# Scan with its bands two rounds ahead, and projections that begin with the receptance, in a hybrid RWKV-7 / attention step

## What is computed

```python
dx = centred_shift(h) - h                      # 0.5 * (left + right neighbour) - h
xr, xw, xk, xv, xa, xg = [h + dx * mu[n] for n in range(6)]
r = heads(xr @ w_r); k_raw = xk @ w_k; v = heads(xv @ w_v); g = sigmoid(xg @ g1) @ g2
for d in range(2):                             # both directions, 16 heads of 64
    decay, a, k_d = ...                        # from xw, xa and k
    def step(S, inp):
        sa = einsum('bhij,bhj->bhi', S, a_t)
        S = S * w_t[..., None, :] + v_t[..., :, None] * k_t[..., None, :] + sa[..., :, None] * b_t[..., None, :]
        return S, einsum('bhij,bhj->bhi', S, r_t)
```

## Time and profile before

| | us |
|---|---|
| median of 3 timed runs | 1508.85 |
| lowest and highest of them | 1502.84, 1514.56 |
| the profiled execution, its own time | 1497.86 |
| span of the profiled execution, first to last instruction | 1496.1 |
| PE busy | 1276.4 (85%) |
| DVE, POOL, ACT busy | 527.0, 387.4, 325.4 |
| mean granted PE clock | 0.92 of 2.4 GHz |

### The profile page before, as it was taken

How to read it: one execution, slowest core, us unless ns; L and a number is a source line. 1 busy time by engine, 2 the same in 40 slices (tenths; PEclk the granted TensorE clock), 3 DMA queues, 4 the chain that set the end, 5 groups by cost and what they waited for, 6 DMA issues and landing times. The chain is left out here.

```text
span 1496.1 us, 21672 instructions
## 1 busy us (share of the span) xinstructions
PE 1276.4 (85%) x8627; PEld 894.2 (60%) x8627; DVE 527.0 (35%) x1159; ACT 325.4 (22%) x801; POOL 387.4 (26%) x708
## 2 busy tenths in 40 slices
PE   4699979999999888799577798979997794888897
PEld 2355845877888777535344455655685452555656
DVE  2800066556655654363510011320025525011115
ACT  2100153332222220031311111111116403111111
POOL 0100065554455432100024223000006601233310
PEclk9899988999999988589789999979997996999997
DMA  9922034766566224206369977847220073877752
GB/s 327 305 94 103 1 122 152 218 212 193 161 212 210 55 62 138 102 1 232 124 256 401 366 261 272 291 100 162 85 85 0 2 285 121 312 261 264 262 186 85
DMA packets 200852, 264.80 MB, mean 177 GB/s; under 512 B 93771, under 2 KB 155611, under 8 KB 185136
## 3 DMA queue, kind: packets, MB, share of 16 engines
q1 hardware_dynamic: 163200, 221.63, 44.2%
q0 software_dynamic: 17152, 31.20, 5.7%
q10 hardware_dynamic: 20400, 10.59, 3.3%
HBM read 300.22 MB, written 28.96 MB: 220 GB/s over the span
## 5 line engine op out<-in xcount | busy, mean ns | idle before, releaser
L2016 PE MATMUL psum<-ring,slab 128*64 128x256 f32 x896 | 192.7, 397 | 34.1 <-DMA slab<-moe_w,slab 31.7
L2016 PE MATMUL psum<-slab 128*64 128x256 f32 x832 | 174.0, 385 | 0.0
L2016 PEld LDWEIGHTS psum<-ring,slab 128*64 128x64 f32 x896 | 117.0, 144 | 94.1 <-issue 54.9
L2016 PEld LDWEIGHTS psum<-slab 128*64 128x64 f32 x832 | 108.1, 139 | 3.6 <-issue 1.0
L2044 PE MATMUL psum<-ring,ws 128*64 128x512 f32 x224 | 94.1, 595 | 17.1 <-issue 15.2
L2189 DVE TENSOR_TENSOR ws<-ws,psum 128x256 f32<-128x256 f32 (+1 forms) x28 | 17.1, 612 | 229.6 <-PE psum L2016 229.6
L2260 PE MATMUL psum<-slab,ring 128*128 128x384 f32 x256 | 85.5, 498 | 7.2 <-PEq L172 7.2
L2453 POOL TENSOR_SCALAR ws<-ws 128x384 f32<-128x384 f32 x32 | 39.4, 1243 | 190.8 <-DVE ws L2523 190.8
L2044 PE MATMUL psum<-slab,ws 128*64 128x512 f32 x208 | 87.5, 598 | 1.3 <-issue 1.3
L2108 POOL DMA_INDIRECT y_rows<-slab x26 | 26.4, 1015 | 228.1 <-DVE slab L2199 228.1
L622 PE MATMUL psum<-slab,ring 128*128 128x384 f32 x256 | 82.7, 486 | 0.0
(11 more groups left out here) (360 smaller groups left out, 2356.5 us busy)
## 6 DMA issues: line engine op xcount, KB each, us to landing
ring<-moe_w SPq DMA_DIRECT2D x84, 1024.0 KB, 7.0
ring<-ada_w SPq DMA_DIRECT2D x46, 1024.0 KB, 9.6
ws<-inverses SPq DMA_DIRECT2D x48, 256.0 KB, 4.0
slab<-moe_w SPq DMA_DIRECT2D x12, 1024.0 KB, 8.5
ring<-na_w_qkv SPq DMA_DIRECT2D x12, 1024.0 KB, 8.1
slab<-y_rows SPq DMA_DIRECT2D x12, 512.0 KB, 6.3
ring<-rwkv_w_r SPq DMA_DIRECT2D x4, 1024.0 KB, 8.4
ring<-rwkv_w_k SPq DMA_DIRECT2D x4, 1024.0 KB, 6.7
```

Source lines behind the costliest of these rows:

```text
L2016: last = nc.tensor.matmul(k.psum[BT * g:BT * g + BT, h_bank(s, kind), 0:DE], cols_[s % 2][:, c, BT * g:BT * g + BT], w[g][:, c, :], start= ...
```

## The change

- **Inputs:** `mean` is one column now, set by a memset; `omu` = 1 - mu is computed, and mu is halved.
- **Projections:** the order is r, w, a, g, k, v. A mix is (1 - mu) h + (mu / 2)(left + right): ACT makes the first product (`prepare`), DVE adds the second. DVE and POOL make the sums for four chunks each. For r, PE goes chunk by chunk over all eight PSUM banks. The four pieces of `w_r` stand ahead of the small ones in the ring.
- **Scan, order:** `bands(r + 2)` stands at the end of round r, behind the outputs and ahead of `modulate(r + 1)`, and in bank + 2 of each direction instead of bank + 1. `scaled_first` is split in `scaled_ar` and `scaled_kb`, for round r + 2, in the gaps of DVE behind the two levels. ACT's exponentials for them stand between its copies of R and U. `modulate(r + 1)` closes round r instead of `modulate(r + 2)`, so the last is at the end of round 8 (before: 7).
- **Scan, opening:** `modulate(1)` goes, `bands(1)` comes; sums of squares and rates are interleaved otherwise; the centring of chunks 4 to 7 moves behind the second scaling.
- **Buffers:** POOL's scratch and one solution get buffers of their own, so that waits fall away; `band` moves to the region that `rate` uses, so POOL's `rates` wait for the band's way out.

```diff
-    plan += [lora_in, gate_in]
-    for n in ("rwkv_w_r", "rwkv_w_k", "rwkv_w_v"):
+    plan += [whole(cols(a["rwkv_w_r"][0], j)) for j in range(4)] + [lora_in, gate_in]
+    for n in ("rwkv_w_k", "rwkv_w_v"):
...
+    def add_sides(ops, lo, hi, sem):
+
+        for t0, t1_ in ((0, CTX), (CTX, T)):
+            ops.tensor_tensor(both[:, lo:hi, t0 + 1:t1_ - 1], h[:, lo:hi, t0:t1_ - 2], h[:, lo:hi, t0 + 2:t1_], ALU.add).then_inc(sem, 1)
...
-            n = 0
-            for t0, t1_ in ((0, CTX), (CTX, T)):
-                nc.vector.tensor_tensor(dx[:, :, t0 + 1:t1_ - 1], h[:, :, t0:t1_ - 2], h[:, :, t0 + 2:t1_], ALU.add).then_inc(step, 1)
...
+            add_sides(nc.vector, 0, 4, step)
             dve.wait_ge(step, 6)
-            for g in range(2):
-                nc.vector.scalar_tensor_tensor(dx[:, 4 * g:4 * g + 4, :], dx[:, 4 * g:4 * g + 4, :], 0.5,
-                                               h[:, 4 * g:4 * g + 4, :], ALU.mult, ALU.subtract).then_inc(step, 1)
-            dve.wait_ge(step, 8)
-            for i, mu in enumerate(MIX_ORDER):
-                if i >= 2:
-
-                    dve.wait_ge(proj, i - 1 if i < 5 else 11)
+            for i, mu in enumerate(MU):
                 for c in range(DC):
-                    nc.vector.scalar_tensor_tensor(mix[i % 2][:, c, :], dx[:, c, :], k.vec[:, V_MU + 8 * mu + c:V_MU + 8 * mu + c + 1],
-                                                   h[:, c, :], ALU.mult, ALU.add).then_inc(mixed, 1)
+                    if i == 0 and c == 4:
+                        dve.wait_ge(step_late, 6)
+                    dve.wait_ge(prepared, DC * i + c + 1)
+                    nc.vector.scalar_tensor_tensor(mix[i][:, c, :], both[:, c, :], k.vec[:, V_MU + 8 * mu + c:V_MU + 8 * mu + c + 1],
+                                                   mix[i][:, c, :], ALU.mult, ALU.add).then_inc(mixed, 1)
...
-            for i in range(3):
-                if i != 1:
-                    piece = take_piece(k, pe, first + i // 2)
-                w = piece_cols(piece[:, D * (i % 2):D * (i % 2) + D])
+            wide = [piece_cols(take_piece(k, pe, first + j)) for j in range(4)]
+            for c in range(DC):
+                pe.wait_ge(mixed, c + 1)
+                for o in range(DC):
+                    last = nc.tensor.matmul(bank(o)[:, 0:T], wide[o // 2][:, c, (o % 2) * P:(o % 2) * P + P], mix[0][:, c, :],
+                                            start=c == 0, stop=c == DC - 1)
+                    if c == DC - 1:
+                        last.then_inc(proj, 1)
...
+            def prepare(i):
+
+                if FREE[i]:
+                    act.wait_ge(proj, FREE[i])
+                for c in range(DC):
+                    nc.scalar.mul(mix[i][:, c, :], h[:, c, :], k.omu[:, DC * MU[i] + c:DC * MU[i] + c + 1]).then_inc(prepared, 1)
...
+            prepare(1)
+            prepare(2)
+            for c in range(DC):
+                act.wait_ge(proj, c + 1)
+                nc.scalar.copy(r3[:, c, :], bank(c)[:, 0:T]).then_inc(read_out, 1)
+            prepare(3)
...
             bands(0)
-            rates_in(6, 10)
-            sum_squares(1)
+            pe.wait_ge(nkk_ok, 1)
+            sum_squares(4, 7)
+            rates_in(6, 8)
+            sum_squares(7, DC)
+            rates_in(8, 12)
+            pe.wait_ge(band_ok[0], 2)
             modulate(0)
-            rates_in(10, 12)
             pe.wait_ge(kk_inverse, 2)
-            for d in range(2):
-                pe.wait_ge(band_ok[d], 2)
             casts(2, 4)
...
-            select(0)
-            pe.wait_ge(sel_ok, 1)
-            modulate(1)
+            pe.wait_ge(ada_ok, 1)
+            pe.wait_ge(band_ok[1], 2)
+            bands(1)
             pe.wait_ge(state_ok, 2)
...
                     pairs(b, odd, 1, a_done[d])
-                    if d == 0 and r + 1 < MOD_PAIRS:
-                        select(r + 1)
+                    if d == 0 and r < MOD_PAIRS:
+                        if r == 0:
+                            pe.wait_ge(band_ok[0], 4)
+                        select(r)
                 for d, b in enumerate(D2):
-                    if d == 0 and r + 1 < MOD_PAIRS:
-                        pe.wait_ge(sel_ok, r + 2)
+                    if d == 0 and r < MOD_PAIRS:
+                        pe.wait_ge(sel_ok, r + 1)
+                    pe.wait_ge(band_ok[d], 2 * min(r + 2, len(ROUNDS)))
                     pairs(b, odd, 0, a_done[d])
-                if (step, q) != LAST:
-                    bands(r + 1)
...
-                if r + 2 < MOD_PAIRS:
-                    modulate(r + 2)
+                if r + 2 < len(ROUNDS):
+                    bands(r + 2)
+                if r + 1 < MOD_PAIRS:
+                    pe.wait_ge(band_ok[0], 2 * min(r + 3, len(ROUNDS)))
+                    modulate(r + 1)
...
                     act.wait_ge(r_done[d], r + 1)
                     nc.scalar.copy(b.r.rearrange("p (e c) n -> p e (c n)", e=2), k.psum[:, b.bank:b.bank + 2, 0:P]).then_inc(r_ok[d], 1)
+                    if r + 2 < len(ROUNDS):
+                        exps(d, *place(r + 2, d), (0,))
                 for d, b in enumerate(D2):
                     act.wait_ge(u_done[d], r + 1)
-                    if (step, q) != LAST:
-                        act.wait_ge(band_out[d], 32 * r + 64)
                     nc.scalar.copy(b.u.rearrange("p u n -> p (u n)"), k.psum[:, b.bank + 2, 0:256]).then_inc(u_ok[d], 1)
+                    if r + 2 < len(ROUNDS):
+                        exps(d, *place(r + 2, d), (2,))
                 if step == 0:
                     for d, b in enumerate(D2):
                         act.wait_ge(s_done[d], r + 1)
                         if q:
                             act.wait_ge(s_out[d], 32 * q)
                         nc.scalar.copy(b.s_ctx.rearrange("p c n -> p (c n)"), k.psum[:, b.bank + 1, 0:P]).then_inc(s_copied[d], 1)
+                if r + 2 < len(ROUNDS):
+                    band_copy(r + 2)
...
+                ahead = r + 2 < len(ROUNDS)
+                if ahead:
+                    scaled_ar(0, r + 2)
+                    scaled_ar(1, r + 2)
+                    scaled_kb(0, r + 2)
                 for d, b in enumerate(D2):
                     dve.wait_ge(half_done[d], r + 1)
                     nc.vector.tensor_copy(b.r[b.late].rearrange("p u n -> p (u n)"), k.psum[b.late, b.bank + 1, 0:256]).then_inc(half_ok[d], 1)
+                if ahead:
+                    scaled_kb(1, r + 2)
                 for d, b in enumerate(D2):
                     dve.wait_ge(late_done[d], r + 1)
                     late = b.u[b.late].rearrange("p u n -> p (u n)")
...
-            scans(2, 6)
+                scaled_rest(d, *place(0, d), 0)
+            scans(2, 4)
+            centre(1)
             floor(1)
+            scans(4, 6)
+            invert(1)
             scans(6, DC)
-            invert(1)
-            centre(1)
             divide(1)
+            dve.wait_ge(nkk_ok, DC)
+            for d in range(2):
+                scaled_ar(d, 1)
+                scaled_kb(d, 1)
+            centre(2)
             dve.wait_ge(state_turned, 1)
             dve.wait_ge(edges_ok, 4)
```

More of the change, by code:

```diff
@@ L332, in _ @@
             nc.gpsimd.memset(k.eps[:], EPS).then_inc(sig_c, 1)
+            nc.gpsimd.memset(k.mean[:], 1.0 / D).then_inc(sig_c, 1)
         @block.tensor
@@ new lines, in _ @@
+            for c in range(DC):
[5 more added lines that the diff above has]
+                        last.then_inc(proj, 1)
+            for j in range(4):
+                k.used[first + j] = (proj, 2 * j + 2)
+            o = DC
@@ L606, in _ @@
+            for i in range(1, 4):
+                if i != 2:
+                    piece = take_piece(k, pe, first + 4 + i // 2)
+                w = piece_cols(piece[:, D * ((i - 1) % 2):D * ((i - 1) % 2) + D])
+                pe.wait_ge(read_out, o - 7)
                 for c in range(DC):
-                    pe.wait_ge(mixed, 8 * i + c + 1)
-                    last = nc.tensor.matmul(bank(i)[:, 0:T], w[:, c, :], mix[i % 2][:, c, :], start=c == 0, stop=c == DC - 1)
+                    pe.wait_ge(mixed, DC * i + c + 1)
+                    last = nc.tensor.matmul(bank(o)[:, 0:T], w[:, c, :], mix[i][:, c, :], start=c == 0, stop=c == DC - 1)
@@ L609, in _ @@
                 last.then_inc(proj, 1)
[L610 to L626 removed]
+                o += 1
@@ new lines, in _ @@
+            k.used[first + 4], k.used[first + 5] = (proj, DC + 2), (proj, DC + 3)
+            for j in range(4):
+                n = first + 6 + j
+                w = piece_cols(take_piece(k, pe, n))
+                for m in range(2):
+                    pe.wait_ge(read_out, o - 7)
+                    for c in range(DC):
+                        if j == 0 and m == 0:
+                            pe.wait_ge(mixed, 4 * DC + c + 1)
+                        last = nc.tensor.matmul(bank(o)[:, 0:T], w[:, c, m * P:(m + 1) * P], mix[4][:, c, :],
```

(7 more changed lines are left out.)

254 lines of the change are left out of this document (118 added, 136 removed).

## The result

Four executions of the changed kernel took 1518.2 to 1539.16 us, median 1536.98; four of the kernel before 1500.47 to 1514.56, median 1505.84. The ratio is 1.020, 95% interval 1.014 to 1.027. I had forecast 1496.0 (range 1480 to 1516): the sign is wrong, and the time lies outside.

What follows compares the result with a forecast made beforehand. PE was the bound, waiting for DVE before the projections and for DVE and inverses in rounds 9 to 11, where its clock falls; 6.8 + 3.2 + 3.3 + 23.9 - 19.2 - 5.2 = 12.8 us won, so 1496.0 us, range 1480 to 1516.

Steps and rivals of the forecast that it cites:

- the clock in the sum: TensorE's clock in the scan: no fall counted in rounds 1 to 8; 12.3 us won in round 11, 2.8 in round 9.
- Rounds 8 to 11: Last scan rounds: round 8 loses 5.2 us at its seam, rounds 9 to 11 win 23.9 us.
- Rival B: Scan: three PE holes per round lower the clock in round 0 and the last rounds; 18.5 us lost, 1527 us; chance 0.12.
- Seams: Between rounds: bands before modulate and a wait for two of four copies cost 2.4 us each, 19.2 lost in rounds 0-7.
- Rival C: Between rounds: copies come early or waits are counted twice, so seams cost 1.6 - 0.3 us; 1487 us; chance 0.20.
- Structure of rounds 0 to 11: Scan apart from the clock: 24.4 us lost at seams, less 3.3 and 8.8 won, so 12.3 us lost.
- rival D: Scan: the bands' lead brings nothing, inverses stay late, rounds 9 to 11 keep about 8 us of waits; 1504 us; chance 0.04.
- Opening: Start of the scan: modulate(1) leaves, bands(1) enters, DVE's chain shortens; product L989 of round 0 comes 3.2 us earlier.
- rival A: Opening of the scan: PE idles and its clock stays low through round 0; 3.4 us lost, 1512 us; chance 0.14.
- The long addition of 2.60 us: Scan opening, solve(0): one POOL addition beside DVE's long centring, otherwise 0.3 us; moving the centring wins 2.6 us net.
- Start: Inputs and projections: 1.5 us from the memset replacing the DMA of mean, 5.3 from an earlier first matmul; 6.8 us won.
- the sides: Projections' neighbour sums: DVE makes half in 1.87 us instead of all in 3.74, POOL makes the others.

Runs made afterwards that it cites:

- seam filled: Changed kernel with three extra unused products in each round's seam, where TensorE waits 0.81 us for the bands' copy; 1516.31 us, ratio 1.007.
- middle filled: Changed kernel with four extra unused products in the 0.95 us hole between the first two level 0 products of every round; 1498.42 us, ratio 1.000.
- the hole alone in the kernel before: Kernel before, first level product of direction 0 on VectorE done four times instead of once, making a mid-round hole; 1540.5 us, ratio 1.023.
- half filled kernel: Changed kernel with two extra unused products in the 0.95 us hole in the middle of every round; 1511.99 us, ratio 1.004.
- the wide selection: The filled kernel with the narrow selection, its four selection products writing each result 16 times (64 columns instead of 4); 1477.63 us, ratio 0.982.
- the filled kernel with the narrow selection: Changed kernel, waits filled by four-column row selection and extra products or removed by reordering, all neighbour sums on VectorE; 1485.78 us, ratio 0.990.

## Why the prediction was wrong

- **The step that failed** is the clock in the sum. In rounds 1 to 8 I let it stand at full speed without a word, since before it had never fallen there; and in "Rounds 8 to 11" I took 12.3 us for round 11 "if the clock holds" and 2.8 for round 9. That is 15.1 us won; measured were 30.0 lost. These 45.1 us, of the 51.1 between forecast and profiled execution (12.8 won, 38.3 lost), decide it. From my own sum I could have seen it: I wrote that L989 cannot begin before DVE's masks and the level product end, 7.85 us after the round, and did not ask what PE does in the last microsecond of that.
- **Rival B** had the mechanism and the place, "about 1 us between L979 and L989", but three holes at once, and the price only for round 0 and the last rounds: 1527 us, with a chance of 0.12. The runs single out the middle hole (seam filled 1516, middle filled 1498, the hole alone in the kernel before +34 us), and it also acts in rounds 1 to 8. My argument against B, that round 10 did not fall, was weak: the hole drops the clock in some rounds only.
- **Seams:** 2.4 us each forecast, 2.42 measured (6.97 - 4.55); the wait for two of four copies was read rightly. Rival C falls.
- **Structure of rounds 0 to 11:** forecast 12.3 us lost (24.4 for seams, less 3.3 and the 8.8 of rounds 9 to 11 that are not the clock's), measured 13.0. No inverse is waited for in the changed kernel's first profile, and 0.40 us in round 11 of the second; rival D falls.
- **Opening:** 2.7 won for 3.2. Round 0 recovered; rival A falls. POOL's operations beside DVE's scans were held up, as forecast: nine of the first ten of solve(0) took 0.76 to 0.99 us, the eighteen behind them 0.21 to 0.29. The long addition of 2.60 us that I counted from the kernel before was one of two there; the next, at 230.46 us, took 2.50.
- **Start:** 5.7 won for 6.8, and that so close by luck. The term mis-sized was the sides: 1.87 us of DVE, if the halves don't slow each other. They do: 4.7 us beside POOL's half, 2.1 without it, so that this part won 2.7 us for 5.3. The memset brought 2.5 us for 1.5 in this execution, above my bound of 1.6; over thirteen profiled executions with the changed inputs the stage starts at 39.86 to 41.77 us, and this one is the earliest. The Trainium skill (SBUF — State Buffer, "SBUF: two separate sides") says that a DVE operation with two SBUF inputs and a GpSimd one that reads SBUF hold each other up for a whole instruction. I had cited that for POOL's long addition and not applied it to this term; the trace agrees with it here too: DVE's first sum took 1.55 us beside POOL's sum and 0.68 without it.
- **Open:** which rounds a given hole hits, and why the median of the changed kernel was 1537 us in one job and 1511 in another (mean clock 0.900 to 0.902 in three of the first four executions, 0.911 to 0.918 in the second four); whether the length of the hole decides how often the clock falls, for which the profiled executions speak and the median of the half filled kernel does not.

## What to carry to other kernels

When a change takes filler work out of a stretch of small products, read from the other engine's rows where the next wait will open, and price it not by its length but by what a clock at half speed costs behind it: here 0.95 to 1.28 us of waiting cost 1.4 to 11.5 us in each round that was hit. Look at the clock line and at the duration of one repeated instruction (2.00 or 3.62 us) before explaining a lost microsecond in any other way. Where a hole can't be removed, work that is needed anyway, and wide, belongs in it; failing that, useless work is cheaper than the hole. It can narrow the spread between executions as well (15 us with the middle filled, 8 us with the wide selection), but did not always: the filled kernel with the narrow selection spread over 40 us.

## What the runs showed of the hardware

- An engine that counts as busy can lose its clock: the selection's 8 passes of 4 columns took 1.01 us and the clock fell behind them in three rounds; 8 passes of 64 columns took 1.06 us and it fell in none (one profiled execution each). Apart from where ACT then reads the result, the two kernels differ in nothing else (1485.8 against 1477.6 us).
- A copy of 4 columns on VectorE took 1.84 us beside a GpSimd sum of 1016 columns, and 0.17 us without it.
- Time and granted clock go together: the kernel with the wide selection had 0.929 to 0.932 in all six executions, which lay 8 us apart. The kernel before, in the same job, had 0.904 and 0.905 in its two longest (1530.51 and 1523.48 us) and 0.916 to 0.923 in the other nine (1500.77 to 1511.9 us).
